# First attention's queries normalised, roped and turned in another order, and six maxima fillings moved into the attention's slots

## What is computed

```python
q = partial_rope(rms_norm(q.reshape(B, S, N_HEADS, HEAD_DIM), q_g), cos, sin)
gates = jax.nn.sigmoid(gl + gate_b).reshape(B, S, N_KV, GQA, 3)
k_cmp = partial_rope(rms_norm(compress(kc, 0), k_g[0]), cos_c, sin_c)
v_cmp = compress(vc, 1)
# per query block, three branches, each a masked softmax
p_cmp = masked_softmax(einsum(qc, k_cmp) * scale, m_cmp)
p_slc = masked_softmax(einsum(qc, kg_sel) * scale, m_slc)
p_win = masked_softmax(einsum(qc, kwc) * scale, m_win)
o = gc[..., 0:1] * o_cmp + gc[..., 1:2] * o_slc + gc[..., 2:3] * o_win
y = (o * silu(z)) @ w_out
x = x + gate * y
```

## Time and profile before

| what | us |
|---|---|
| median of 3 runs | 959.11 (955.93 to 961.8) |
| the profiled execution's own time | 957.23 |
| its span, first to last instruction | 955.4 |
| PE busy in the span | 900.7 |
| DVE busy | 571.8 |
| ACT busy | 489.4 |
| POOL busy | 172.9 |

### The profile page before, as it was taken

How to read it: one execution, slowest core, us unless ns; L and a number is a source line. 1 busy time by engine, 2 the same in 40 slices (tenths; PEclk the granted TensorE clock), 3 DMA queues, 4 the chain that set the end, 5 groups by cost and what they waited for, 6 DMA issues and landing times.

```text
span 955.4 us, 12987 instructions
## 1 busy us (share of the span) xinstructions
PE 900.7 (94%) x4989; PEld 772.8 (81%) x4989; DVE 571.8 (60%) x917; ACT 489.4 (51%) x764; POOL 172.9 (18%) x188
## 2 busy tenths in 40 slices
PE   2799898999799999999999999999999999999998
PEld 2588787899678988888888888888888788888886
DVE  5974586545766637755555446767455755555542
ACT  3334573556355564654444437586664565445431
POOL 1015344355116340100000002452000010000000
PEclk9799898999989999999999999999999999999999
DMA  9955645254646245555655565553325565555650
GB/s 369 319 180 177 221 151 180 84 143 145 203 157 196 84 138 177 176 180 193 192 189 194 173 176 180 162 155 111 97 81 154 159 213 180 176 180 193 200 176 22
DMA packets 45692, 163.26 MB, mean 171 GB/s; under 512 B 5184, under 2 KB 5440, under 8 KB 45632
## 3 DMA queue, kind: packets, MB, share of 16 engines
q1 hardware_dynamic: 45632, 162.44, 53.2%
HBM read 161.37 MB, written 1.05 MB: 170 GB/s over the span
## 4 chain that ended last, share of the span: by engine, by line
PE 85%; DVE 8%; ACT 3%; issue 2%; DMA 1%; POOL 1%; SPq 0%; DVEq 0%; ACTq 0%
PE bank L482 57%; PE bank L491 11%; PE bank L506 4%; DVE w_lo L1526 2%; PE bank L639 2%; DVE mx L1677 1%; DVE ada_acc L1624 1%; PE bank L645 1%; PE bank L722 1%; PE bank L665 1%; PE bank L667 1%; PE bank L666 1%; DMA w_raw<-in_weights 1%; ACT kh L1031 1%; DVE qs L1779 1%
## 5 line engine op out<-in xcount | busy, mean ns | idle before, releaser
L1027 ACT ACTIVATE w_hi<-w_raw 128x1024 fp32r<-128x1024 f32 (+2 forms) x249 | 259.2, 1046 | 185.2 <-PE bank L482 159.1
L1526 DVE TENSOR_TENSOR w_lo<-w_raw,w_hi 128x1024 fp32r<-128x1024 f32 (+2 forms) x249 | 302.0, 1231 | 81.5 <-ACT w_hi L1027 80.9
L482 PE MATMUL bank<-w_hi,h_hi 128*128 128x512 f32 (+1 forms) x576 | 229.7, 399 | 10.9 <-ACT h_hi L1031 6.3
L482 PE MATMUL bank<-w_hi,h_lo 128*128 128x512 f32 (+1 forms) x576 | 225.4, 391 | 0.0
L482 PE MATMUL bank<-w_lo,h_hi 128*128 128x512 f32 (+1 forms) x576 | 225.3, 391 | 0.0
L482 PEld LDWEIGHTS bank<-w_hi,h_hi 128*128 128x128 f32 x576 | 109.7, 190 | 33.7 <-issue 12.7
L482 PEld LDWEIGHTS bank<-w_hi,h_lo 128*128 128x128 f32 x576 | 109.4, 190 | 22.9
L482 PEld LDWEIGHTS bank<-w_lo,h_hi 128*128 128x128 f32 x576 | 109.7, 190 | 21.1
L2290 POOL TENSOR_TENSOR ada_acc<-ada_acc,w_raw 128x512 f32<-128x512 f32 x56 | 78.0, 1394 | 100.6 <-ACT w_raw L1031 95.3
L491 PE MATMUL bank<-h_hi,w_hi 128*128 128x256 f32 x264 | 79.3, 300 | 3.3 <-DVE tokq L1606 3.1
L491 PE MATMUL bank<-h_lo,w_hi 128*128 128x256 f32 x264 | 76.6, 290 | 0.0
(11 more groups left out here) (296 smaller groups left out, 1366.8 us busy)
## 6 DMA issues: line engine op xcount, KB each, us to landing
w_raw<-in_weights SPq DMA_DIRECT2D x298, 512.0 KB, 3.8
w_raw<-in_weights SPq DMA_DIRECT2D x4, 360.0 KB, 3.3
x<-in_x SPq DMA_DIRECT2D x1, 1024.0 KB, 6.9
gate_row<-in_gate_bias SPq DMA_DIRECT2D x2, 512.0 KB, 7.0
out<-x SPq DMA_DIRECT2D x4, 256.0 KB, 3.2
w_raw<-in_weights SPq DMA_DIRECT2D x3, 256.0 KB, 2.8
const<-in_constants SPq DMA_DIRECT2D x1, 413.5 KB, 8.3
cols<-in_columns SPq DMA_DIRECT2D x1, 208.5 KB, 2.5
```

Of the source, the lines that this page charges most:

```text
L482: mm = e.matmul(pb[t][:, 0:n], xs[q], ws[p], start=(k + kk == 0 and i == 0), stop=(k + kk == kts - 1 and i == 2))
L1027: e.activation(w_hi[i % NSPLIT][:, 0:c], raw[v % NRAW][:, 0:c], ACT.Copy).then_inc(*rounded(v))
L1526: e.tensor_tensor(w_lo[i % NSPLIT][:, 0:c], raw[v % NRAW][:, 0:c], w_hi[i % NSPLIT][:, 0:c].bitcast(F32), ALU.subtract).then_inc(*rested(v))
```

## The change

Nothing is computed differently. Three things move.

1. *The norm of the second q half.* On ACT the squares of `nsa_q1` stand ahead of the eight `kh` copies instead of behind them, and one more weight unit is rounded between. DVE's four `kl` rests go behind the sums of `nsa_q1`. POOL ropes q0's second half before q1's power.
2. *The turns of q.* q0 is turned right behind `nsa_gate`, into banks 7 and 1; q1 is turned inside `nsa_vsvw` behind its third unit, into banks 5 and 7. Their copies and rests move along. `nsa_z0` gets a wait for q0's last rest, since bank 1 is now used.
3. *Fillings 18 to 23.* `nsa_z1` has two fillings behind each of its first three units and none behind the fourth (six instead of twelve). Fillings 18 to 23 move into the hooks of slots 1, 2 and 3, two each, in banks 2 and 3, where the first ones wait for `z_done`. Fillings 0 and 4 use bank 6 instead of 7.

The core of the diff:

```diff
-        for s, per, branches, order in (("nsa", 2, slice(0, 2), (7, 2, 3, 4)), ...
+        for s, per, branches, order in (("nsa", 2, slice(0, 2), (6, 2, 3, 4)), ...
...
-                bank = (7, 4)[n % 2] if s == "nsa" and n > 7 else order[n % 4]
+                bank = order[n % 4] if s == "moba" or n < 8 else (7, 4)[n % 2] if n < 18 else 2 + n % 2
...
             whole(linear("nsa_gate", 0, (h_hi, h_lo), h_of(0), False, [hn_scaled.at(("nsa_q1", 1, 0))]))
+            q_turns("nsa_q0", 0, banks[7], modulated.at((0, 3)))
+            q_turns("nsa_q0", 1, banks[1], hn_scaled.at(("nsa_q1", 1, 0)))
...
                 if j == 2:
-                    q_turns("nsa_q0", 1, banks[4], gates_done.at())
...
+                    q_turns("nsa_q1", 0, banks[5], kc_placed.at())
+                    q_turns("nsa_q1", 1, banks[7], heads_placed.at(("nsa_q0", 0)))
+            first = {0: vc_done.at(3), 1: v_done.at(("nsa", 1)), 2: v_done.at(("nsa", 1)), 3: gates_done.at(),
+                     8: heads_placed.at(("nsa_q1", 1)), 18: z_done.at(("nsa_z1", 1)), 19: z_done.at(("nsa_z1", 1))}
...
-                for n in range(12 + 3 * j, 15 + 3 * j):
+                for n in range(12 + 2 * j, 14 + 2 * j) if j < 3 else ():
                     maxima_scores("nsa", n, filling_free("nsa", n, first))
...
+                if i in (1, 2, 3):
+                    for n in range(16 + 2 * i, 18 + 2 * i):
+                        maxima_scores("nsa", n, filling_free("nsa", n, first))
...
-                if j == 3:
-                    k_places("nsa_kskw", "nsa_ks", 0, banks[4])
-                    k_places("nsa_kskw", "nsa_kw", 1, banks[6])
-            head_squares("nsa_q1", hn_summed.at(("nsa_q0", 1)))
-            for j, u in enumerate(of["cmp_w1_1"]):
-                rounds(u)
+            head_squares("nsa_q1", hn_summed.at(("nsa_q0", 1)))
+            for j, u in enumerate(of["cmp_w1_1"]):
+                rounds(u, 4)
+                if j == 0:
+                    k_places("nsa_kskw", "nsa_ks", 0, banks[4])
+                    k_places("nsa_kskw", "nsa_kw", 1, banks[6])
...
                 if j == 0:
+                    head_sums("nsa_q1")
+                if j == 2:
                     k_rests("nsa_kskw", "nsa_ks", 0, banks[4])
                     k_rests("nsa_kskw", "nsa_kw", 1, banks[6])
-                    head_sums("nsa_q1")
                 if j == 3:
                     head_scales("nsa_q1")
...
-                maxima("nsa", 12 + 3 * j, 13 + 3 * j, 14 + 3 * j)
+                if j < 3:
+                    maxima("nsa", 12 + 2 * j, 13 + 2 * j)
...
+                if step_ == 1 and i in (1, 2, 3):
+                    maxima("nsa", *range(16 + 2 * i, 18 + 2 * i))
```

More of the change, by code:

```diff
@@ L401, in program @@
         fillings, slots = {"nsa": [], "moba": []}, {"nsa": [], "moba": []}
-        for s, per, branches, order in (("nsa", 2, slice(0, 2), (7, 2, 3, 4)), ("moba", 4, slice(0, 1), (6, 7, 4, 5))):
+        for s, per, branches, order in (("nsa", 2, slice(0, 2), (6, 2, 3, 4)), ("moba", 4, slice(0, 1), (6, 7, 4, 5))):
             nb = branches.stop
@@ L623, in filling_free @@
                 for m in range(n - 1, -1, -1):
-                    if fillings[s][m]["bank"] == fillings[s][n]["bank"]:
+                    if fillings[s][m]["bank"] == fillings[s][n]["bank"] and n not in first:
                         return m_reduced.at((s, m))
@@ L776, in tensor @@
                                     for tt in range(TT)]).then_inc(*gates_turned())
-                    q_turns("nsa_q0", 0, banks[5], kc_placed.at())
                 if j == 2:
-                    q_turns("nsa_q0", 1, banks[4], gates_done.at())
-            first = {0: modulated.at((0, 3)), 1: v_done.at(("nsa", 1)), 2: v_done.at(("nsa", 1)),
-                     3: heads_placed.at(("nsa_q0", 1))}
-            for j in linear("nsa_z0", 0, (h_hi, h_lo), h_of(0), False, [gate_biased.at()]):
-                if j == 0:
-                    q_turns("nsa_q1", 0, banks[6], vc_done.at(3))
-                if j == 1:
-                    q_turns("nsa_q1", 1, banks[5], heads_placed.at(("nsa_q0", 0)))
+                    q_turns("nsa_q1", 0, banks[5], kc_placed.at())
+                    q_turns("nsa_q1", 1, banks[7], heads_placed.at(("nsa_q0", 0)))
+            first = {0: vc_done.at(3), 1: v_done.at(("nsa", 1)), 2: v_done.at(("nsa", 1)), 3: gates_done.at(),
+                     8: heads_placed.at(("nsa_q1", 1)), 18: z_done.at(("nsa_z1", 1)), 19: z_done.at(("nsa_z1", 1))}
+            for j in linear("nsa_z0", 0, (h_hi, h_lo), h_of(0), False, [gate_biased.at(), heads_placed.at(("nsa_q0", 1))]):
                 for n in range(3 * j, 3 * j + 3):
@@ L793, in tensor @@
                     compressed_scores(j, (banks[5], banks[6]),
-                                      (c_masked.at(0) if j else heads_placed.at(("nsa_q1", 1)),))
+                                      (c_masked.at(0) if j else m_reduced.at(("nsa", 7)),))
                 if j == 2:
@@ L801, in tensor @@
             o_two = lambda s: lambda k: [o_rounded.at((s, k // 2)), o_rested.at((s, k // 2))]
-            outs = [linear("nsa_out0", 1, (o_hi, o_lo), o_two("nsa"), True, [z_done.at(("nsa_z1", 1))]),
+            outs = [linear("nsa_out0", 1, (o_hi, o_lo), o_two("nsa"), True, [z_done.at(("nsa_z1", 1)), m_reduced.at(("nsa", 23))]),
                     linear("nsa_out1", 2, (o_hi, o_lo), o_two("nsa"), True, [exped.at(("nsa", 7, 1, 1))])]
@@ L817, in tensor @@
             pair_attention("nsa", [v_done.at(("nsa", 1)), pc_done.at(1), zeroed.at(3)],
-                           [[m_reduced.at(("nsa", 23)), c_masked.at(1)], [m_reduced.at(("nsa", 23)), pc_done.at(0)],
+                           [[m_reduced.at(("nsa", 17)), c_masked.at(1)], [m_reduced.at(("nsa", 17)), pc_done.at(0)],
                             lambda pr: ada_cols.at(5 + pr) if pr else gate_row_done.at(5)], nsa_hook)
@@ L1269, in scalar @@
                         copy(vc[gs, g, :], banks[6][gs, 0:HD]).then_inc(*vc_done(g))
-                if j == 2:
-                    q_places("nsa_q0", "nsa_q", 0, banks[5])
+                if j == 0:
+                    q_places("nsa_q0", "nsa_q", 0, banks[7])
+                    q_places("nsa_q0", "nsa_q", 1, banks[1])
                 if j == 3:
-                    q_places("nsa_q0", "nsa_q", 1, banks[4])
+                    q_places("nsa_q1", "nsa_q", 0, banks[5])
             for tt in range(TT):
@@ L1278, in scalar @@
                 rounds(u, 4)
-                if j == 1:
-                    q_places("nsa_q1", "nsa_q", 0, banks[6])
-                if j == 2:
-                    q_places("nsa_q1", "nsa_q", 1, banks[5])
+                if j == 0:
+                    q_places("nsa_q1", "nsa_q", 1, banks[7])
                 scale_chunk(4, j)
@@ L1917, in vector @@
                 rests(u)
+                if j in (0, 1):
+                    q_rests("nsa_q0", "nsa_q", j, banks[(7, 1)[j]])
                 if j == 3:
-                    q_rests("nsa_q0", "nsa_q", 0, banks[5])
+                    q_rests("nsa_q1", "nsa_q", 0, banks[5])
                 if j == 2:
@@ L1969, in vector @@
                 if j == 0:
-                    q_rests("nsa_q0", "nsa_q", 1, banks[4])
-                if j == 2:
-                    q_rests("nsa_q1", "nsa_q", 0, banks[6])
-                if j == 3:
-                    q_rests("nsa_q1", "nsa_q", 1, banks[5])
+                    q_rests("nsa_q1", "nsa_q", 1, banks[7])
                 maxima("nsa", 3 * j, 3 * j + 1, 3 * j + 2)
@@ L2305, in gpsimd @@
             e.tensor_copy(kc2[:, 1, :], kc2[:, 0, :]).then_inc(*kc_doubled())
+            head_ropes("nsa_q0", 1)
             head_power("nsa_q1")
-            head_ropes("nsa_q0", 1)
             head_ropes("nsa_q1")
```

## The result

| | before | after |
|---|---|---|
| median, us | 958.72 (20 runs, 955.1 to 961.8) | 960.6 (20 runs, 958.32 to 961.91) |
| ratio after/before | | 1.0025 (95%: 1.0013 to 1.0037) |
| the profiled execution's own time | 957.23 | 959.37 |
| its span | 955.4 | 957.6 |

The changed kernel is 0.25% slower, where 953.9 us and a gain of 0.5% had been forecast. 960.6 lies outside the range of 948.5 to 959.5. So the loss is small, 0.5 to 1.9 us by the medians; what both comparisons show is that the forecast gain is missing.

The account below looks back on a forecast made before the run. PE was taken as the bound, busy 900.7 of 955.4 us. Terms of -9.35 + 0.7 + 2.3 + 2.05 = -4.3 us, set against 958.2, gave 953.9 us (chance 0.45), range 948.5 to 959.5.

Parts of the forecast that it names:

- step 5: Slot 1 of the attention: the clock falls behind the new 2.04 us wait, 2.05 us lost, bounds 0 and 2.84.
- the sum: Whole kernel: -9.35 + 0.7 + 2.3 + 2.05 = -4.3 us, giving 953.9 us.
- Step 1: Ahead of `nsa_gate`: DVE's order keeps the scaling late, 0.7 us lost, bounds 0 and 1.2; wait of 3.5 to 4.2.
- Rival C: Ahead of `nsa_gate`: the wait and its half clock go away, 6.1 us less, 947.8 us; chance 0.07.
- Step 2: q's transposes around `nsa_z0`: PE's work is the same, no new wait is charged, DVE's reductions are relieved.
- Step 3: Fillings 0 to 17 ahead of the attention: all waits but one of 0.65 us go, 9.35 us saved.
- Rival E: Fillings: remainders or reductions come late, half of the 9.35 us stays as waits, 958.6 us; chance 0.12.
- Step 4: Fillings 18 to 23 in slots 1 to 3: new 2.04 us wait for `z_done`, 2.3 us lost, bounds 1.5 and 3.3.
- rival D: Attention: half clock holds on over the narrow values, slower than before past 14 us, 20 us give 960.9; chance 0.07.
- rival B: Slot 1: the clock holds behind the new wait, 2.05 us come back, 951.8 us; chance 0.24.
- I expect it to reach the end: Behind the change: PE is the bound and transfers were done early, so the saving was expected to reach the kernel's end.

Follow-up runs that it names:

- e5: Changed kernel with DVE's scaling of `nsa_q1` ahead of the four `kl` rests and `w_lo1` instead of behind them: 945.09 us, ratio 0.9844.
- e2: Changed kernel with PE's gate-row matmul of slot 1 issued three times, filling most of the 2.04 us wait: 952.34 us, ratio 0.9923.
- e1: Changed kernel with DVE's two products of `nsa_z1` done in slot 0 of the attention instead of slot 1: 948.36 us, ratio 0.9887.
- e9: Changed kernel with chunk 4's gate-row matmul issued three times, 1.84 us more PE work ahead of the attention: 951.88 us, ratio 0.9928.
- e7: Changed kernel with filling 18 waiting for the first of the two products of `nsa_z1` instead of the second: 957.71 us, ratio 0.9973.
- e10: Changed kernel with the scaling of `nsa_q1` ahead of the `kl` rests and 1.84 us of added PE work ahead of the attention: 955.38 us, ratio 0.996.
- e3: Kernel before with part 3 of the change only, but fillings 0 and 4 staying in bank 7: 956.05 us, ratio 0.9959.
- e11: Changed kernel with fillings 18 and 19 behind slot 1's last values instead of ahead of them: 949.17 us, ratio 0.9897.
- e6: Changed kernel with the products of `nsa_z1` in slot 0 and the scaling of `nsa_q1` ahead of the `kl` rests: 945.37 us, ratio 0.9841.
- e4: Kernel before with parts 1 and 2 of the change only, and fillings 0 and 4 in bank 6: 957.71 us, ratio 0.9981.

## Why the prediction was wrong, step by step

The waits and what ends them came as forecast. The step that failed is step 5, the price of the half clock in slot 1: taken as 2.05 us, it measured 6.4. On top came 2 us far behind the change, for which the sum had no term.

**Step 1, the wait ahead of `nsa_gate`: right.** 0.7 us lost was forecast; from `cmp_w1_1` to the gate it is 10.38 before and 11.07 after, and the wait is 3.76 in the band of 3.5 to 4.2. The scaling stands right behind a `w_lo`. e5 showed the cause: with the scaling ahead of the rests it ran at 100.69, 5.8 us after `cmp_w1_1`'s start, where the reading of the chain had 6.0 (99.7 less 93.70), and the wait was gone. Rival C was a true account of what holds the gate; it was not what this change does.

**Step 2, the turns: right.** The waits after show none of q's transposes and no new one of a unit (the 1.8 of L482 is that of the earlier trace rows), and without parts 1 and 2 filling 11's wait is 1.7 instead of 0.6.

**Step 3, fillings 0 to 17: right.** Of 9.35 us plus 2.3 of moved work (11.65), 12.1 came, 0.17 of the difference from `nsa_gate` itself (5.05 us where it took 5.22). The other 0.3 is not traced. The remaining wait was 0.63 where 0.65 was taken, a number picked between 0.44 and 1.75, so there is luck in how well it fits. Rival E did not happen.

**Step 4, the wait in slot 1: right.** 2.04 us measured, 2.04 forecast; wait and restart together are 2.3, as e2 against e1 gives. The upper bound of 3.3 was not needed. The 0.07 for the signal had no row behind it; here it is 0.05 (the products end at 174.72, the filling starts at 174.77). POOL added from 172.93 to 178.45 in this stretch, and the two products beside it took 1.27 us, as in the earlier trace rows. By the lock of the Trainium skill (SBUF — State Buffer, "SBUF: two separate sides") a whole addition could have held a step of the chain with two SBUF inputs. The one such step, the multiplication of `factors` and `gates`, took 0.80 us for its two instructions beside an addition, and 0.79 before; no longer hold shows, and the other steps, which read a bank or a single tile, do not test the rule. The moved work came out as 1.9, not 2.3.

**Step 5, the clock in slot 1: the term that was mis-sized.** It was taken as 2.05, midway of 1.3 and 2.84, and measured 6.4 (44.02 against 37.59 and 37.60 with the same wait and no fall, in e5 and e9). The price of a slow microsecond, 0.45, was about right: 13.6 us of low clock cost 6.4, which is 0.47. What was wrong was the length. The text bounded it by the three low stretches of before, all over within 7.4 us, and gave 0.07 to rival D, in which it holds on over the narrow values and eats the gain once it passes 14 us. The whole trace of before would not have warned of it either: cut into stretches of 1 us, it has no longer low stretch anywhere. Behind the wait in slot 1 the clock stayed low for 13.6 to 13.7 us in five traces (the changed kernel three times, e7, e10). The case of no fall (rival B) is also real: e5 and e9 have the same wait without one. So the term was never one number between 1.3 and 2.84, but one of at least three outcomes: 0, 3.2 (e3) and 6.4. What ended the low clock after 6.8 us in e3 and after 13.6 here is open.

**The sum.** From `cmp_w1_1` to slot 4 the steps had -4.3 us in all (with the moved 2.3 us taken out of one stretch and put into the next) and the traces have -0.8: the clock cost 4.35 more, while 0.45 more was saved ahead of the attention and the moved work came out 0.4 smaller. Behind slot 4 come 0.5 us saved up to MoBA's turns and 2.1 lost in the last stretch, which takes 640.2 to 640.5 in the three traces of the changed kernel and 638.2 before. At 742 us, ahead of the next projection, PE waits 2.7 us for DVE in both kernels, and only in the changed one does the clock fall there. The timeline and stretch of before, then of after:

```profile
742.00 0.47 PE L482 MATMUL bank<-w_hi,h_hi 128*128 128x512 f32 x1 [2.65 <-DVE h_lo L2205]
...
742.00:745.40 3.40, 3.40 (x15) 2.83 (x16) 3.33 (x6) 1.01 (x2) 0.00 (x0) 1.00 0.12 48
```

```profile
742.68 0.76 PE L482 MATMUL bank<-w_hi,h_hi 128*128 128x512 f32 x1 [2.68 <-DVE h_lo L2207]
...
742.68:746.08 3.40, 3.40 (x9) 2.68 (x10) 3.33 (x6) 1.03 (x2) 0.00 (x0) 0.54 0.07 28
```

Nine matmuls where fifteen ran: 1.6 us by 0.47 a microsecond, the most of the 2. No step had an entry for this, since nothing there is changed. It is no mark of the changed kernel alone: e7, e10 and e11 have the fall at this wait too. e7 and e11 lose little by it (638.7 and 638.6), since they lack another low stretch of 3.4 us, which before has at 324.3 and the changed kernel at 326.0. Together the traces make the changed kernel 0.8 us slower behind `cmp_w1_1`, which lies between the 1.9 and the 0.5 us of the two comparisons; the rest is the start and the spread of single executions, which the traces do not settle. The step "I expect it to reach the end" was true of the work and false of the clock, which gave and took at places that the change does not touch.

**The rule of the Trainium skill that stood with rival B** (TensorE: Matmul & The Clock Gate, "HAM oscillation") warns only of idle gaps longer than those in slot 1; by it the 2.04 and 1.43 us waits would have left the clock alone. In six of the eight traces that have such a wait the clock fell, so there the traces disagree with it. The section had already missed the falls of before, and should have weighed nothing for B.

**What stays open.** Why the same wait lets the clock fall in one place and not 1.6 us later, and why the low stretch is then 6.8 us in one kernel and 13.6 in another. e9 and e10 show that time alone, without any other difference near the wait, flips the outcome; they do not show what it is counted from. It is not the span's start: the three traces of the changed kernel begin `cmp_w1_1` at 95.11, 95.71 and 97.42 us, and all have the same low stretch. Nor is it settled whether the later start of the changed kernel in its profile (95.11 against 93.70) is more than the spread of starts.

## What to carry to other kernels

A new wait on PE has two prices: its length, which the trace gives well (2.04 forecast and measured here), and its clock, which is a matter of cases and not of a midpoint. Work out the worst case too (here the low stretch was about twice as long as any that the trace of before had shown), and weigh it before trusting a gain of the same size. Since the clock's answer flips with a shift of 2 us, judge an edit by its waits and by more than one placement, not by one time alone: e9 makes the kernel "faster" by adding work.

It is safer to remove such waits than to price them. Here each repair was a reordering on an engine that executes in order: DVE's late product moved to where DVE is idle (948.36 us), the waiting fillings put behind ready work on PE (949.17), and the critical scaling put ahead of queued rests (945.09, ratio 0.9844, 1.6% below the kernel before). All three beat both kernels, and the last one, with or without the first, is the fastest. With the scaling alone, though, 6.4 of its us rest on where the wait in slot 1 happens to fall: that wait is still there, and the same kernel with 1.8 us of added work ahead of it (e10) takes 955.38. With both repairs (e6, 945.37) the wait itself is gone.

## What the runs showed of the hardware

- A wait of 2.04 us on PE was followed by 13.6 to 13.7 us at 1.2 GHz (the changed kernel three times, e10), by 6.8 to 7.1 (e3), or by none (e5, e9). One of 1.43 us was followed by 13.6 (e7), one of 1.79 by 6.8 (e4), where 1.75 was followed by none (before), one of 2.65 to 2.68 at 742 us by none or by 3.4.
- PE had no idle time during the low stretch in slot 1 (14.00 busy of 14.00), so a full engine alone did not bring the clock back for those 13.6 us. The stretch began about 1 us behind the wait's end in the changed kernel (174.77; matmuls at full speed up to 175.7), and almost at once in e3 (the first filling took 0.60).
- A slow microsecond cost 0.45 us over the 256-column matmuls of the gate, and 0.47 over the mix of 64 to 512 columns in slots 1 and 2.
